# A two-layer transformer trunk on one core: chunk limits as two contraction rows and inside the expanded bias, and bias and maximum in one vector pass

## The reference

```python
# layer 0: multi-head latent attention, block-causal by chunks of 64
s = einsum('bqhd,bkhd->bhqk', qblk, k) * scale          # 96 numbers a head
mask = kchunk[None, :] <= qchunk[:, None]
p = softmax(where(mask, s, neg)); o = p @ v
x = x + o @ w_o; x = x + swiglu(rms_norm(x), w1, w3, w2)
k, v = shared_band_kv(x)                                 # for layer 1
# layer 1: each 64-frame chunk sees its own chunk and the 8 before it
s = einsum('bqhd,bkhd->bhqk', qch, kb) * scale + bias    # 64 numbers a head
s = where(valid, s, neg)                                 # bias: rel_bias[h, clip(distance)]
p = softmax(s); o = p @ v
x = x + o @ w_o; x = x + moe_swiglu(rms_norm(x))         # top 2 of 8 experts
```

## Time and profile before

| | |
|---|---|
| median of 3 runs | 1530.07 us (1530.01, 1530.07, 1532.9) |
| profiled execution, own time | 1533.14 us |
| its span in the trace | 1531.2 us |
| TensorE busy | 1457.5 us (95%) |
| VectorE busy | 1156.8 us (76%) |
| ScalarE busy | 954.8 us (62%) |
| first attention, first to last score product | about 84 to 125 us |
| second attention, the same | about 425 to 463 us |

### The profile page before, as it was taken

The page is one execution under the profiler, slowest core; times in us unless marked ns, Lnnn a source line. Parts: engine busy times, 40 slices in busy tenths (PEclk is TensorE's granted clock), DMA queues, the critical chain, the costliest instruction groups (busy, mean ns, idle before and its releaser), DMA issues.

```text
span 1531.2 us, 20154 instructions
## 1 busy us (share of the span) xinstructions
PE 1457.5 (95%) x7313; PEld 1225.2 (80%) x7313; DVE 1156.8 (76%) x1033; ACT 954.8 (62%) x919; POOL 43.6 (3%) x79
## 2 busy tenths in 40 slices
PE   5689899998988899999999999999999999999998
PEld 5578899997876688878878878887887887887886
DVE  4655544456684889879888888988988898888894
ACT  4445443345553677767676777677776777777772
POOL 3120000000100000000000000000000000000000
PEclk9879999999999799999999999999999999999999
DMA  8323455554531589999989999998998999999992
GB/s 292 133 83 106 142 190 180 181 190 149 187 124 64 175 324 381 377 332 342 377 329 347 373 336 339 374 370 308 370 383 324 353 375 328 339 384 338 331 377 89
DMA packets 148448, 424.64 MB, mean 277 GB/s; under 512 B 7981, under 2 KB 38842, under 8 KB 148410
## 3 DMA queue, kind: packets, MB, share of 16 engines
q1 hardware_dynamic: 140448, 417.23, 74.4%
q10 hardware_dynamic: 7578, 6.84, 1.5%
q0 software_dynamic: 384, 0.07, 0.2%
HBM read 423.06 MB, written 4.19 MB: 279 GB/s over the span
## 4 chain that ended last, share of the span: by engine, by line
PE 92%; DVE 4%; ACT 1%; issue 1%; POOL 0%; DMA 0%; ACTq 0%; POOLq 0%; SPq 0%; DVEq 0%
PE ps L1354 81%; PE ps L1349 4%; PE ps L1678 2%; PE ps L1652 2%; PE ps L1468 2%; PE ps L1490 1%; DVE wl_a L909 1%; ACT wh_a L583 0%; DMA xr<-in_x 0%; ACT tn L592 0%; DVE kT L1037 0%; POOL rstd L475 0%; DVE nmax L1050 0%; DVE bias L1047 0%; DVE xr L945 0%
## 5 line engine op out<-in xcount | busy, mean ns | idle before, releaser
L909 DVE TENSOR_TENSOR wl_a<-raw,wh_a 128x2048 fp32r<-128x2048 f32 (+1 forms) x230 | 515.9, 2270 | 121.1 <-ACT wh_a L583 121.1
L583 ACT ACTIVATE wh_a<-raw 128x2048 fp32r<-128x2048 f32 (+1 forms) x230 | 433.9, 1906 | 205.7 <-PE ps L1354 202.1
L909 DVE TENSOR_TENSOR wl_b<-raw,wh_b 128x2048 fp32r<-128x2048 f32 x168 | 378.8, 2287 | 35.5 <-ACT wh_b L583 34.5
L583 ACT ACTIVATE wh_b<-raw 128x2048 fp32r<-128x2048 f32 x168 | 319.3, 1925 | 57.2 <-PE ps L1354 55.9
L1354 PE MATMUL ps<-wh_a,hth 128*128 128x512 f32 (+2 forms) x576 | 225.2, 391 | 6.2 <-DVE htl L928 3.8
L1354 PE MATMUL ps<-wh_a,htl 128*128 128x512 f32 (+2 forms) x576 | 222.4, 386 | 0.0
L1354 PE MATMUL ps<-wl_a,hth 128*128 128x512 f32 (+2 forms) x576 | 222.4, 386 | 0.0
L1354 PE MATMUL ps<-wh_b,hth 128*128 128x512 f32 x448 | 178.4, 398 | 0.0
L1354 PE MATMUL ps<-wh_b,htl 128*128 128x512 f32 x448 | 174.6, 390 | 0.0
L1354 PE MATMUL ps<-wl_b,hth 128*128 128x512 f32 x448 | 174.3, 389 | 0.0
L1354 PEld LDWEIGHTS ps<-wh_a,hth 128*128 128x128 f32 x576 | 108.7, 189 | 30.2 <-issue 7.0
(11 more groups left out here) (233 smaller groups left out, 2103.4 us busy)
## 6 DMA issues: line engine op xcount, KB each, us to landing
raw<-in_moe_w SPq DMA_DIRECT2D x336, 1024.0 KB, 7.2
raw<-in_ffn_w SPq DMA_DIRECT2D x33, 1024.0 KB, 5.1
raw<-in_a_w_o SPq DMA_DIRECT2D x4, 1024.0 KB, 6.0
raw<-in_b_w_q SPq DMA_DIRECT2D x4, 1024.0 KB, 5.1
raw<-in_kv_w_k SPq DMA_DIRECT2D x4, 1024.0 KB, 5.0
raw<-in_kv_w_v SPq DMA_DIRECT2D x4, 1024.0 KB, 5.0
raw<-in_b_w_o SPq DMA_DIRECT2D x4, 1024.0 KB, 4.9
bias<-bias_wide ACTq DMA_DIRECT2D x8, 384.0 KB, 3.1
```

What stands on the lines that cost most here:

```text
L583: nc.scalar.activation(dst[:, 0:w], raw[:, n % RAW, 0:w], ACT.Copy).then_inc(hi_done, 1)
L909: nc.vector.tensor_tensor(l[:, 0:w], raw[:, n % RAW, 0:w], h[:, 0:w].bitcast(fp32), ALU.subtract).then_inc(lo_done, 1)
```

## The change

1. In layer 0 the contraction of the scores grows from 96 to 98 rows. Rows 96 and 97 of `qT` and `kT` hold the chunk limit of query tile 0 and 1: ones for the first 64 queries of that tile, and -2^100 on the last 64 keys that the tile's product reads. SP writes them by eight small transfers from the constants, once TensorE has used the last unit of the latent projections; TensorE waits for all eight before the first scores.
2. In layer 1 the limit is part of the expanded bias. It is built by six transfers instead of two, and SP issues them, between the loads of the first two units of the dense feed-forward and the third.
3. The 64 mask products, the tile `mask` and its copy on ScalarE go.
4. In layer 1 `maxima` is one `tensor_tensor_reduce` for each of the two key ranges: it writes -(scores + bias) and the minimum of that, which is the negated maximum. ScalarE takes the exponential with scale -1. The semaphore `sb` goes; TensorE waits for `nm` instead before it writes a score bank again.
5. VectorE's loop over pairs is written out in layer 1.

```diff
+            sp.wait_ge(unit_used, U_UKV + 2)
+            for tile_, at in ((qT, C_MA), (kT, C_MB - CHUNK)):
+                for r in range(T):
+                    for t in range(T):
+                        dst = tile_[QK + r:QK + r + 1, :, :].rearrange("p a (h t q) -> p (a h) t q", h=2, t=T)[:, :, t, :]
+                        row = 0 if r == t else 1
+                        sp.dma_start(dst, consts[row:row + 1, at:at + P].unsqueeze(1).to_broadcast([1, 4, P])).then_inc(mask_here, 16)
             for w, v in enumerate((w1_v, w3_v)):
                 load(U_FFN + w, v[:, :, 0:FW], (DC, FW))
+            for at, skip, keys in ((0, P, P), (P, 0, SEQ)):
+                for q0, seen in ((0, keys - CHUNK), (CHUNK, keys)):
+                    src = bass.AP(tensor=bias_rows.tensor, offset=P - 1 + skip - q0, ap=[[SPAN, HEADS], [-1, CHUNK], [1, seen]])
+                    sp.dma_start(bias_wide[:, q0:q0 + CHUNK, at:at + seen], src).then_inc(wide_done, 16)
+                sp.dma_start(bias_wide[:, 0:CHUNK, at + keys - CHUNK:at + keys],
+                              bass.AP(tensor=consts.tensor, offset=C_MB,
+                                      ap=[[0, HEADS], [0, CHUNK], [1, CHUNK]])).then_inc(wide_done, 16)
...
-            nc.scalar.activation(mask[:], cst[:, C_MA:C_MA + P + CHUNK], ACT.Copy).then_inc(mask_done, 1)
...
                         last = nc.scalar.activation(prob[:, par, h, lo_:lo_ + n_], src[:, lo_:lo_ + n_], ACT.Exp,
+                                                    scale=1.0 if la == 0 else -1.0,
...
-            for at, skip, keys in ((0, P, P), (P, 0, SEQ)):
-                src = bass.AP(tensor=bias_rows.tensor, offset=P - 1 + skip, ap=[[SPAN, HEADS], [-1, P], [1, keys]])
-                act.dma_start(bias_wide[:, :, at:at + keys], src).then_inc(wide_done, 16)
...
-                        src = bias[:, par, h, :]
-                        nc.vector.tensor_tensor(src, ps[2 + h][:, 0:SPAN], src, ALU.add).then_inc(a["sb"], 1)
-                        dve.wait_ge(a["sb"], p * 2 + (h + 1))
...
+                            b = bias[:, par, h, lo_:lo_ + n_]
+                            last = nc.vector.tensor_tensor_reduce(b, src[:, lo_:lo_ + n_], b, -1.0, 3e38, ALU.add, ALU.min,
+                                                                  nmax[:, par, t, h:h + 1])
...
-                        pe.wait_ge(a["ex" if la == 0 else "sb"], p * 2 + (h - 1))
+                        pe.wait_ge(a["ex" if la == 0 else "nm"], p * 2 + (h - 1))
-                    part = slice(0, QK if la == 0 else P)
+                    part = slice(0, QK + 2 if la == 0 else P)
-                        mm(ps[2 + h][:, lo_:lo_ + keys], qT[...], kT[...], start=True, stop=False)
-                        last = mm(ps[2 + h][:, lo_ + keys - CHUNK:lo_ + keys], mask_row, mask_col, start=False, stop=True)
+                        last = mm(ps[2 + h][:, lo_:lo_ + keys], qT[...], kT[...], start=True, stop=True)
```

More of the change, by code:

```diff
@@ L147, in trunk_kernel @@
         ropt = sb("ropt", [P, 2, 2, T, ROPE])
-        mask = sb("mask", [P, P + CHUNK], f32r)
         negh = sb("negh", [P, T])
@@ L236, in trunk_kernel @@
         number = cst[:, C_E3:C_E3 + V_EXTRA * NE].rearrange("p (i e) -> p i e", e=NE)
-        mask_row = mask[:, 0:P]
-        mask_col = mask[:, P:P + CHUNK]
         q1 = q_all[:, :, 0:D]
@@ L256, in trunk_kernel @@
         c_here = sem("c_here")
-        mask_done = sem("mask_done")
+        mask_here = sem("mask_here")
         g_here = sem("g_here")
@@ L299, in trunk_kernel @@
                 "s",
-                "sb",
                 "nm",
@@ L711, in attention @@
                 if la == 1:
-                    act.wait_ge(wide_done, 32)
+                    act.wait_ge(wide_done, 16 * 6)
                     load_bias(0, 0, wait=False)
@@ L1042, in maxima @@
                     src = ps[2 + h]
-                    if la == 1:
-                        if h == 0:
-                            dve.wait_ge(bias_here[par], (p - par) * 8 + 16)
-                        src = bias[:, par, h, :]
-                        nc.vector.tensor_tensor(src, ps[2 + h][:, 0:SPAN], src, ALU.add).then_inc(a["sb"], 1)
-                        dve.wait_ge(a["sb"], p * 2 + (h + 1))
-                    for t, (lo_, n_) in enumerate(((0, P), (P, SEQ))):
-                        last = nc.vector.tensor_reduce(nmax[:, par, t, h:h + 1], src[:, lo_:lo_ + n_], axis=AX,
-                                                       op=ALU.max, negate=True)
+                    if la == 1 and h == 0:
+                        dve.wait_ge(bias_here[par], (p - par) * 8 + 16)
+                    for t, (lo_, n_) in enumerate(((0, P), (P, SEQ))):
+                        if la == 0:
+                            last = nc.vector.tensor_reduce(nmax[:, par, t, h:h + 1], src[:, lo_:lo_ + n_], axis=AX,
+                                                           op=ALU.max, negate=True)
+                        else:
+                            b = bias[:, par, h, lo_:lo_ + n_]
+                            last = nc.vector.tensor_tensor_reduce(b, src[:, lo_:lo_ + n_], b, -1.0, 3e38, ALU.add, ALU.min,
+                                                                  nmax[:, par, t, h:h + 1])
                     last.then_inc(a["nm"], 1)
@@ L1088, in attention @@
                 step(1, 1)
-                with dve.Fori(1, PAIRS // 2 - 1) as j:
-                    for u in range(2):
-                        step(j * 2 + u, u)
+                if la == 0:
+                    with dve.Fori(1, PAIRS // 2 - 1) as j:
+                        for u in range(2):
+                            step(j * 2 + u, u)
+                else:
+                    for p in range(2, PAIRS - 2):
+                        step(p, p % 2)
                 step(PAIRS - 2, 0, more=False)
@@ L1461, in scores @@
                     if not first:
-                        pe.wait_ge(a["ex" if la == 0 else "sb"], p * 2 + (h - 1))
-                    part = slice(0, QK if la == 0 else P)
+                        pe.wait_ge(a["ex" if la == 0 else "nm"], p * 2 + (h - 1))
+                    part = slice(0, QK + 2 if la == 0 else P)
                     q_at = h * SEQ if la == 0 else 0
                     for t, (lo_, keys) in enumerate(((0, P), (P, SEQ))):
-                        mm(ps[2 + h][:, lo_:lo_ + keys], qT[part, par, q_at + t * P:q_at + (t + 1) * P],
-                           kT[part, par, h * SEQ:h * SEQ + keys], start=True, stop=False)
-                        last = mm(ps[2 + h][:, lo_ + keys - CHUNK:lo_ + keys], mask_row, mask_col, start=False, stop=True)
+                        last = mm(ps[2 + h][:, lo_:lo_ + keys], qT[part, par, q_at + t * P:q_at + (t + 1) * P],
+                                  kT[part, par, h * SEQ:h * SEQ + keys], start=True, stop=True)
                     last.then_inc(a["s"], 1)
@@ L1497, in attention @@
                 yield
-                pe.wait_ge(mask_done, 1)
+                if la == 0:
+                    pe.wait_ge(mask_here, 16 * 8)
                 scores(0, 0, 0, first=True)
```

## The result

The changed kernel takes **1523.1 us** (median of five runs, 1521.37 to 1523.29) against 1530.61 us for the kernel before in the same rounds (five runs, 1530.01 to 1532.9). The ratio is **0.9944, 95% interval 0.9932 to 0.9956**: faster by 0.56%. Forecast were 1520.7 us in 1517 to 1527. The profiled execution after took 1523.13 us with a span of 1521.3 us; the one before 1533.14 and 1531.2. The two traces are thus 9.9 us apart, the forecast sum was 9.4, and the medians are 7.5 us apart; the interval of the ratio is 6.7 to 10.4 us, so it holds the sum. The point on the clock, further down, says how far these differences can be traced.

A forecast was written before the change was run, and what follows sets the result against it. TensorE was taken to bound the run (92% of its chain), with VectorE's `k_out` also in the second attention's loop. Savings of 3.4 and 6.0 us, 9.4 together, gave 1520.7 us against the median of 1530.07; range 1517 to 1527.

The forecast's parts named there:

- Mask products: Both attentions, TensorE: removing a head's two saves 0.21 us; 3.4 us in the first attention, 0.42 a step in the second.
- The pass: Second attention, VectorE: one pass per key range instead of addition and reductions cuts the block before `k_out` from 1.12 to 0.75 us.
- the short ones cost nothing: Lower end for VectorE's block in the second attention: with the short result-writing instructions free, it takes 0.57 us.
- The second attention's step: Second attention's loop: a step falls from 5.26 to 4.47 us, saving 0.79; 6.0 us in all with the ends.
- The sum: Whole run: 3.4 us from the first attention plus 6.0 from the second, 9.4 us saved.
- the kernel is slower: Rival, second attention: the new VectorE instructions are dear, 0.557 us each, giving 1540.6 us; decides from about 1.8 a block; chance 0.04.
- the masks' case: Rival, both attentions: mask products were nearly free, 0.06 us for two, so 3.9 us remain and 1525.2; chance 0.06.
- The bias load: Rival, second attention: the load becomes the bound if it lands 0.5 us later, costing 1.8 in seven steps, 1522.5; chance 0.12.
- Half rate: Rival, second attention: the new VectorE pass runs at half rate, a block takes 1.12 us, total 1523.9; chance 0.15.
- The eight transfers and their wait: Ahead of the first attention: SP's small mask transfers land by 82.2 us at worst, before the first score at 83.82; cost nothing.
- The moved bias transfers: SP's queue ahead of the third feed-forward unit: nothing lost, as SP had a wait of 65 us there.
- The clock: First attention: half clock up to 98 us; a rise moved from there was listed as a sign of being wrong.

The follow-up runs named there:

- r_after: The changed kernel run and profiled again, unedited: 1522.99 us, ratio 0.9939 to the kernel before.
- e5: The changed kernel with its six bias transfers issued on ScalarE's queue instead of SP's: 1541.45 us, ratio 1.0066 to the kernel before.
- e10: e5 with the masked blocks read from 64 different rows of constants instead of the same 256 bytes: 1530.55 us, ratio 0.9997 to the kernel before.
- e2: The kernel before with only the first attention's mask products replaced by mask rows in the contraction: 1532.73 us, ratio 1.0007.
- e6: The kernel before with 13 additional, never-read products in TensorE's pause ahead of the first attention: 1529.31 us, ratio 0.9984.
- e7: The changed kernel with 13 additional, never-read products in TensorE's pause ahead of the first attention: 1521.34 us, ratio 0.9932 to the kernel before.
- e8: e7 with such products also in three later turns and ahead of the router's selection (3, 3, 5 and 3): 1518.11 us, ratio 0.9912.
- e9: e8 with two more products in the first pause and one between first transposes and first scores: 1516.95 us, ratio 0.9910 to the kernel before.

## Why the prediction was right, point by point

- **Mask products.** Direction and mechanism right, size too high. The working took 0.21 us for a head's two; the steps show 4.81 - 4.48 = 0.33 for two heads, **0.165** each, and 0.32 in the second attention too. A mask product is worth 0.08 us, two thirds of the pitch of 0.12 from which the working started. The first attention gave 3.1 at nearly equal clock (forecast 3.4).
- **The pass.** The block was forecast at 0.75 and is **0.56**, at the lower end of 0.57 that was kept for "the short ones cost nothing". The working priced the accumulator's read by a reciprocal of 0.175 less an overlap; it takes 83 ns, all beside the next instruction. The prices of the passes, 0.31 and 0.43, were right within 0.02 (0.292, 0.420).
- **The second attention's step**: 0.32 + 0.55 = 0.87 where 0.42 + 0.37 = 0.79 was forecast. Two errors of opposite sign: 0.10 too much for the masks, 0.18 too little for the pass. Its 6.4 us against 6.0 came a little otherwise than costed: from the second `k_out` to the eighth the six steps took 26.21 us instead of 31.24, 5.0 less, and 0.5 came ahead of them and 0.9 behind them, where 0.5 was forecast for both ends.
- **The sum**: 3.1 + 6.4 = 9.5 against 9.4. That near a match is luck of the signs, not a sign that every term was right. Three small numbers of the working do not come out, and none enters the sum: the masks at half clock are 21 x 0.21 = 4.4 and not 4.5; by its own terms the kernel is slower from a block of 1.5 us on and slower by more than 3 us from 1.7, not 1.8; and the cases that it counts as faster add up to more than 0.85, being 0.87 without the masks' case.
- **The bias load**: not the bound, and the margin was read rightly. Issued at 435.66 and landing 3.2 us later, at 438.9, it is there 0.3 us before the pass at 439.16 (forecast 0.25), and in this profile none of VectorE's waits in the second attention names a DMA. In r_after one does, 0.76 us ahead of the first pass of all; the steps behind it are 4.39 there as well.
- **Half rate**: fell. By the Trainium skill, Vector Engine (DVE) Microarchitecture Reference, section "Points that are easy to get wrong", two SBUF sources that are not bf16 halve the throughput of a scalar-tensor-tensor form; here one source is in PSUM, and 384 columns in two passes take 0.71 us against 0.695 for the two reductions. No run here had two SBUF sources.
- **The eight transfers and their wait**: nothing, as costed. The first score of the first attention waits 0.93 us for `kT`, as it did before; SP had issued the last mask row 10.8 us earlier. Inside the second attention the first score of a step waits 0.44 us for `kT`, where 0.5 was said.
- **The moved bias transfers**: nothing on the path, as costed, but because of the room there, not of the price. The working looked at one price, 2.20 us for two, and at SP's slack of 65 us; 24 us of issues were taken from that slack. e5 shows what the same transfers cost where somebody waits behind them: 18 us.
- **The clock**: the working let it rise at 98 us in both kernels. It rose at 88 and 90 in the changed kernel and at 91 in the second profile of the kernel before, so its own sign of being wrong, a moved rise, says nothing of the change. This is why the trace's difference (9.9) does not confirm the sum (9.4): the first attention's early rise gave some 4 us too much, and the half clock between the attentions took 3.7 back. The profiled execution before lay 3.1 us over the median, and the forecast subtracted that in full; the late rise alone does not explain it, since the second profiled execution, with the early rise, took 1532.56 us as well. The remaining 2 us between the sum and the difference of the medians lie within the interval (6.7 to 10.4 us; 7.2 to 11.6 for r_after). That they are clock is argued from two profiles of each kernel, and not shown.

## What to carry to other kernels

Price a small product that is taken out of a pipelined row by less than the pitch of its starts, and a pass that replaces two by the pass of its size alone, its accumulator's read at nothing where another instruction follows. When transfers are moved to another queue, ask not only whether that queue has room but what the same transfers cost if a waiting engine must issue them: here that was the difference between 0.6% faster and 0.7% slower. And before a gain is put down to a change, profile the kernel before a second time: the stretch at half clock behind a pause was 27.3 us long in one execution and 17.1 in another of the same program. Compare distances between two instructions there, not moments: ahead of the first attention, where the program was the same, the moments of two profiles lay 1.6 us apart.

## What the runs showed of the hardware

- **A repeated source is slow.** Behind the first transfer that reads the same 256 bytes over and over, the core's DMA moved 17 GB/s from 84 to 91 us in the changed kernel, and a bias transfer of 1024 KB landed 29.8 us after its issue. With the source spread over 64 rows it moved 217 GB/s from 91 to 98 us, against 18 in e5, and six issues took 9 us less (e10).
- **An issue can hold its engine for microseconds.** Issues of one kind took 0.45 and 4.75 us (e2), 0.5 to 7.1 us (e5). In both rows the first is the shortest and the later ones are long; what makes them long was not separated.
- **The clock behind a pause is not a function of the program alone.** In two profiles of the kernel before, with the same pause ahead and TensorE busy 6.07 to 7.00 of each 7 us, it was 0.50 from 91 to 98 in one and 0.99 in the other. With the pause filled but for 1.91 us, and 0.93 left behind the transposes, it still fell (e6: 0.52 from 84 to 91; e7 and e8 too); with 0.19 and 0.50 left it did not (e9, one profile).
- **Products that compute nothing can pay**, in time when TensorE stands still: with them the changed kernel's ratio to the kernel before went from 0.9939 (r_after) to 0.9910 (e9), 4.4 us; the medians, from different chips, are 6.0 us apart.
